# A decoder layer on one core: the block sums of the feed-forward weights are formed during attention and during the up product instead of during the input projection

## What is computed

```
z  = rmsnorm(x) @ w_in                      # 1024 x 3120
a  = GLA heads, sparse attention heads (three branches), mLSTM heads, from z
x  = x + concat(a) @ w_out                  # 1024 x 1024
x  = x + relu(rmsnorm(x) @ w_up)^2 @ w_down # 1024 x 4096, 4096 x 1024
```

## Time and profile before

| | us |
|---|---|
| Timed runs | 1925.2, 1925.57, 1929.59 (median 1925.57) |
| Profiled execution, its own time | 1918.35 |
| Its span, first to last instruction | 1916.6 |
| Projection | 0 to 517 |
| Attention | 517 to about 760 |
| Other mixers and the decoded samples | about 760 to 1110 |
| Output projection | about 1113 to 1228 |
| Up phase | about 1228 to 1573 |
| Down phase | about 1573 to the end |

### The profile page before, as it was taken

How to read it: one execution, slowest core, us unless ns; L and a number is a source line. 1 busy time by engine, 2 the same in 40 slices (tenths; PEclk the granted TensorE clock), 3 DMA queues, 4 the chain that set the end, 5 groups by cost and what they waited for, 6 DMA issues and landing times. The chain is left out here.

```text
span 1916.6 us, 34635 instructions
## 1 busy us (share of the span) xinstructions
PE 1694.0 (88%) x13909; PEld 1558.6 (81%) x13909; DVE 1091.9 (57%) x1814; ACT 736.7 (38%) x1379; POOL 261.9 (14%) x276
## 2 busy tenths in 40 slices
PE   7725998678799999799999779779999989999998
PEld 6625997678688888678876369779999989999998
DVE  6305326521278777556667775876666675545542
ACT  6311223110166555544445432343333343333331
POOL 1101000000122222332221132410000000000000
PEclk9866998798889999899999789989999999999999
DMA  7998889999941001357749756236556578665652
GB/s 171 151 300 202 154 165 283 283 225 204 226 100 24 2 2 44 117 202 244 235 148 271 167 171 196 75 117 218 175 186 189 182 247 285 184 200 185 196 174 62
DMA packets 339037, 333.61 MB, mean 174 GB/s; under 512 B 62190, under 2 KB 272710, under 8 KB 336254
## 3 DMA queue, kind: packets, MB, share of 16 engines
q1 hardware_dynamic: 309102, 226.20, 41.4%
q0 software_dynamic: 27392, 100.67, 20.0%
q10 hardware_dynamic: 2384, 4.53, 0.7%
HBM read 261.50 MB, written 141.15 MB: 210 GB/s over the span
## 5 line engine op out<-in xcount | busy, mean ns | idle before, releaser
L59 PE MATMUL pm<-ops,slots 128*128 128x258 f32 x1792 | 511.1, 285 | 26.6 <-DVE ops L3694 19.5
L60 PE MATMUL pm<-ops,slots 128*128 128x258 f32 x1792 | 509.4, 284 | 0.0
L61 PE MATMUL pm<-ops,slots 128*128 128x258 f32 x1792 | 508.3, 284 | 0.0
L59 PEld LDWEIGHTS pm<-ops,slots 128*128 128x128 f32 x1792 | 340.6, 190 | 27.6 <-DVE ops L3694 20.2
L61 PEld LDWEIGHTS pm<-ops,slots 128*128 128x128 f32 x1792 | 342.9, 191 | 0.0
L60 PEld LDWEIGHTS pm<-ops,slots 128*128 128x128 f32 x1792 | 342.8, 191 | 0.0
L59 PE MATMUL pz<-hH,winH 128*128 128x344 f32 x600 | 209.9, 350 | 60.7 <-DVE zb L910 59.0
L3521 ACT ACTIVATE slots<-uact 128x512 fp32r<-128x512 f32 x224 | 137.4, 626 | 172.7 <-DMA uact<-upS_scratch 48.0
L60 PE MATMUL pz<-hL,winH 128*128 128x344 f32 x600 | 201.8, 336 | 0.0
L61 PE MATMUL pz<-hH,winL 128*128 128x344 f32 x600 | 201.0, 335 | 0.0
L3700 DVE TENSOR_TENSOR slots<-uact,slots 128x512 fp32r<-128x512 f32 x224 | 156.5, 708 | 75.5 <-ACT slots L3521 75.4
(11 more groups left out here) (671 smaller groups left out, 3232.5 us busy)
## 6 DMA issues: line engine op xcount, KB each, us to landing
hidD_scratch<-onat SPq DMA_DIRECT2D x112, 258.0 KB, 3.8
upS_scratch<-in_w_up_dram POOLq DMA_DIRECT2D x12, 2048.0 KB, 21.5
downS_scratch<-in_w_down_dram POOLq DMA_DIRECT2D x12, 2048.0 KB, 17.1
hs<-hidD_scratch SPq DMA_DIRECT2D x38, 516.0 KB, 4.8
uact<-upS_scratch SPq DMA_DIRECT2D x64, 256.0 KB
uact<-downS_scratch SPq DMA_DIRECT2D x64, 256.0 KB
raw<-in_w_in_dram SPq DMA_DIRECT2D x24, 512.0 KB, 14.9
uact<-in_w_up_dram SPq DMA_DIRECT2D x48, 256.0 KB
```

The costliest lines, as they stand in the source:

```text
L59: nc.tensor.matmul(out, wH, mH, start=start and k == 0, stop=False)
L60: nc.tensor.matmul(out, wH, mL, start=False, stop=False)
L61: last = nc.tensor.matmul(out, wL, mH, start=False, stop=stop and k == n - 1)
```

## The change

All of the sums leave the projection. The sums of `w_up` are issued by POOL at the beginning of attention, behind the masks and before the first scaling step: four copies (eight DMAs) and the first adds of sums 0 and 1 there, the adds of sums 2 and 3 at the sliding steps one half and three quarters of the way through. The sums of `w_down` are issued by POOL in `mix_and_mixer` behind `x_fourth(1)`, when the second half's operands have been split; SP waits for each of them only where the down phase loads its first unit. The pacing by `raw_in` is gone. For `w_down` the rows are at most 512 bytes instead of 2048 (`max_dma_last_dim` counts bytes).

```diff
@@ project_and_prepare, gpsimd @@
-                for which in range(2):
-                    ...
-                    slot(1)
-                    begin(0, block_of(1, 0))
-                    slot(2)
-                    begin(1, block_of(0, 0))
-                    slot(3)
-                    begin(2, block_of(0, 0))
-                    slot(4)
-                    begin(3, block_of(0, 1))
-                    for n in range(2):
-                        slot(5 + n)
-                        add(0, n, block_of(1, 1))
-                    ...
@@ attend_prompt, gpsimd @@
+                def copy_sum(f, block):
+                    for n in range(2):
+                        rows = slice(n * 256, (n + 1) * 256)
+                        nc.gpsimd.dma_start(io["upS"][f, rows, :], block[rows, :], max_dma_last_dim=2048).then_inc(sums_done[f], 16)
+
+                def add_sum(f, block):
+                    pool.wait_ge(sums_done[f], 32)
+                    for n in range(2):
+                        rows = slice(n * 256, (n + 1) * 256)
+                        nc.gpsimd.dma_start(io["upS"][f, rows, :], block[rows, :], accum_op=ALU.add, max_dma_last_dim=2048).then_inc(sums_done[f], 16)
+                ...
+                copy_sum(0, up_quarter(1, 0))
+                copy_sum(2, up_quarter(0, 0))
+                copy_sum(1, up_quarter(0, 0))
+                copy_sum(3, up_quarter(0, 1))
+                add_sum(0, up_quarter(1, 1))
+                add_sum(1, up_quarter(1, 0))
+                sliding = [s for s in range(len(sched.steps)) if sched.steps[s][1] == WIN]
                 for s in range(len(sched.steps)):
+                    if s == sliding[len(sliding) // 2]:
+                        pool.wait_ge(sums_done[0], 64)
+                        add_sum(2, io["upS"][0])
+                    if s == sliding[3 * len(sliding) // 4]:
+                        pool.wait_ge(sums_done[2], 64)
+                        add_sum(3, io["upS"][2])
                     if s == ahead_at:
                         gather_ahead()
@@ mix_and_mixer, sync @@
                 def load_weights(n):
                     ...
+                    if n >= NUP and (n - NUP) % 16 == 0 and (n - NUP) // 16 in SUM_OF:
+                        sp.wait_ge(down_summed[SUM_OF[(n - NUP) // 16]], 64)
@@
                 for n in range(4):
-                    sp.wait_ge(late_sums[0][n], 64)
+                    sp.wait_ge(late_sums[n], 64)
@@
-                for n in range(4):
-                    sp.wait_ge(late_sums[1][n], 64)
@@ mix_and_mixer, gpsimd, behind x_fourth(1) @@
                 pool.wait_ge(xL_ready, 14)
+                ...
+                def copy_sum(f, block):
+                    for n in range(2):
+                        rows = slice(n * D, (n + 1) * D)
+                        nc.gpsimd.dma_start(io["downS"][f, rows, :], block[rows, :], max_dma_last_dim=512).then_inc(down_summed[f], 16)
+                (add_sum the same way, with accum_op=ALU.add and a wait for the sum's copy)
+
+                copy_sum(0, down_quarter(1, 0))
+                copy_sum(2, down_quarter(0, 0))
+                add_sum(0, down_quarter(1, 1))
+                copy_sum(1, down_quarter(0, 0))
+                pool.wait_ge(down_summed[0], 64)
+                add_sum(2, io["downS"][0])
+                copy_sum(3, down_quarter(0, 1))
+                add_sum(1, down_quarter(1, 0))
+                pool.wait_ge(down_summed[2], 64)
+                add_sum(3, io["downS"][2])
```

More of the change, by code:

```diff
@@ L77 @@
 QK_ROWS = (4, 5, 0, 1, 2, 3)
-SUM_ROW = 2048
 def project_and_prepare(nc, io, keep):
@@ L86, in project_and_prepare @@
     xTd = io["xT"].rearrange("(k p) t -> p k t", p=P)
-    w_up, w_down = io["w_up"].rearrange("l d n -> (l d) n"), io["w_down"].rearrange("l f n -> (l f) n")
     zT, zS = io["zT"], io["zS"]
@@ L1347, in _, with up_quarter @@
                 nc.gpsimd.memset(cmask[:, :, NB:P], -BIG).then_inc(masks, 1)
+                sums_done, w_up = keep["weight_sums"], io["w_up"].rearrange("l d n -> (l d) n")
+                def up_quarter(i, j):
+                    return w_up[j * 512:(j + 1) * 512, i * 2 * D:(i + 1) * 2 * D]
+                def copy_sum(f, block):
[7 more added lines that the diff above has]
+                        nc.gpsimd.dma_start(io["upS"][f, rows, :], block[rows, :], accum_op=ALU.add, max_dma_last_dim=2048).then_inc(sums_done[f], 16)
                 def scale_sliding(s):
@@ L3084, in mix_and_mixer @@
         acc_in = [sem(f"acc_in{m}") for m in range(NM)]
+        down_summed = [sem(f"down_summed{n}") for n in range(4)]
         smp_ready, out_t, out_a, ys_t, ys_a = (sem(n) for n in ("smp_ready", "out_t", "out_a", "ys_t", "ys_a"))
@@ L3335, in _, with down_quarter, add_sum @@
                 pool.wait_ge(xL_ready, 14)
+                w_rows = io["w_down"].rearrange("l f n -> (l f) n")
+                def down_quarter(i, j):
+                    return w_rows[j * 2 * D:(j + 1) * 2 * D, i * 512:(i + 1) * 512]
+                def copy_sum(f, block):
+                    for n in range(2):
+                        rows = slice(n * D, (n + 1) * D)
+                        nc.gpsimd.dma_start(io["downS"][f, rows, :], block[rows, :], max_dma_last_dim=512).then_inc(down_summed[f], 16)
+                def add_sum(f, block):
+                    pool.wait_ge(down_summed[f], 32)
+                    for n in range(2):
+                        rows = slice(n * D, (n + 1) * D)
+                        nc.gpsimd.dma_start(io["downS"][f, rows, :], block[rows, :], accum_op=ALU.add, max_dma_last_dim=512).then_inc(down_summed[f], 16)
+                copy_sum(0, down_quarter(1, 0))
[8 more added lines that the diff above has]
+                add_sum(3, io["downS"][2])
                 for j in FINAL:
@@ L3941, in program @@
             keep["late_z"] = nc.alloc_semaphore("late_z_stored")
-            keep["weight_sums"] = [[nc.alloc_semaphore(f"sums_{which}{n}") for n in range(4)] for which in ("up", "down")]
+            keep["weight_sums"] = [nc.alloc_semaphore(f"up_sums{n}") for n in range(4)]
             project_and_prepare(nc, io, keep)
```

## The result

The changed kernel took 1906.9 us in the median of five runs (1895.28 to 1916.99), the kernel before 1925.57 (1923.12 to 1930.35). The forecast of 1919 with 1870 to 1990 holds it, 12 us too high. The spans of the two profiled executions differ by 23.0 us, and all that follows takes that difference apart.

The account below looks back on a forecast made before the run. It took `raw` loads sharing DMA engines with the sums to bound the projection, PE attention and the up phase. -110 + 33 + 3 + 67 = -7 us gave 1911, or 1919 on the median's scale; range 1870 to 1990.

Parts of the forecast that it names:

- Step 1: Projection: without the sums its `raw` loads quicken and PE sets the pace, -110 us (bounds -130 to -75).
- The dear bound: Projection: the least gain, -75 us, if all 44 us of other waits stay and DVE adds 20.
- Step 2: Start of attention: POOL held until sum 1's copy lands, +33 us, and +3 for later adds.
- The hold: Start of attention: POOL's first scaling delayed by waiting for sum 1's copy, 32 us, taken as 33.
- the two later pairs: Attention: two later pairs of adds stop POOL 3.5 us each, mostly hidden, +3 us (0 to 7).
- Step 3: Up phase: packets of the `w_down` sums take turns with SP's weight loads, +67 us.
- loss less cover: Up phase, copies: loss of 37 us, less 11 us covered by units split ahead.
- loss less joins: Up phase, accumulates: loss of 49 us, less 8 for software-queue gaps at the joins of the chain.
- Accumulates of 2 KB: Rival, up phase: accumulates not made smaller or as dear as large ones, loss 97 to 134 us; chance 0.25.
- Copies that shrink: Rival, up phase: copy packets shrink too and cost nothing, loss about 20 to 38 us; chance 0.17.
- Another chain in the projection: Rival: `store_qk`, DVE's order or output stores keep slots near 14 us, return only 75, sum +28; chance 0.08.

Follow-up runs that it names:

- e5: Changed kernel with the first adds of `w_up` sums 0 and 1 moved to the 9th and 17th sliding step: 1858.21 us, ratio 0.9724 to the kernel before.
- e1: Changed kernel with all sums left out, plain quarters read instead (output not the layer's): 1790.1 us, ratio 0.9329 to the kernel before.
- e9: Changed kernel without `w_up` sums and with only the eight copies of the `w_down` sums, no adds: 1823.26 us, ratio 0.9511 to the kernel before.
- e4: Changed kernel with rows of 2048 instead of 512 bytes for the `w_down` sums: 1945.67 us, ratio 1.0129 to the kernel before.
- e3: Changed kernel with the `w_up` sums left out, plain quarters read instead: 1864.48 us, ratio 0.9724 to the kernel before.
- e6: Kernel before with 512-byte instead of 2048-byte rows in its accumulates, all sums still in the projection: 1954.22 us, ratio 1.0202.
- e7: Kernel before with `w_up` sums spread over projection slots (512-byte accumulate rows), `w_down` sums over attention's sliding steps, none in the up phase: 1798.54 us, ratio 0.9395.

## Why the prediction came out as it did

**What bounded the kernel** was read rightly: with the sums gone, `raw` lands in 3.6 us and PE is full.

**Step 1, -127.5 against -110.** The mechanism was right, the term mis-sized. The work of PE was put at 285 and measured at 288.45; the 25 us of waits that I kept on top of it are 3.5 us (292 - 288.45). Those waits in the profile before (9.1, 8.0, 7.5, 19.7) went with the sums, all but a few microseconds, although none of them was named for a DMA. The value lies inside the bounds of -130 to -75, near the end that I did not take. This term is more than the whole error of -16 in the span. (The dear bound has a slip: 285 + 44 + 20 against 420 is -71, not -75.)

**Step 2, +37.6 against +36.** Right in its cause: the adds behind the wait for sum 1's copy were issued at 446.2, 56.7 behind the masks, and PE waited 40.0 us for it; e5 takes the wait away and gets all of it back. That the size is right too is partly luck, since two misses cancel. The hold was put too low: the first scaling came 39 us later than before (58.7 behind the masks, not 19.5), where 32 stood. A pair took 10 x 16 / 606 = 0.264 us in 415:425, not 0.204, and 6 x 32 of them make 51 us; sum 1's copy landed 52.7 us after POOL began (393.2 to 445.9), where 44 stood. SP's packets there were of 1.13 MB / 605 = 1.9 KB: the query and key loads have rows of 4 KB and 2 KB (8 and 4 times 128 elements, line 3910 of the kernel before), not of 512 bytes as the section on attention says. And the 3 us for the two later pairs are not seen: e5 has them too and its stretch is e1's.

**Step 3, +65.3 against +67.** Right in its mechanism and, partly by luck, in the sum; the 65.3 are also those of the fastest run. The pair of an accumulate was put at 0.093 and measured at 0.0937. The parts were off against each other: the copies cost 35 to 37 us by e9 where loss less cover made 26, the accumulates 34 to 41 where loss less joins made 41. The copies' transfers took longer than 55 us, from 1134 to 1202 in e9, at 0.240 a packet in place of 0.215, though SP passed 1.6 packets for each, not one. All transfers took 309 us and not the forecast 245: POOL issued the second of a pair only when the first had landed, so there was a gap of the software queue at each of them. SP never waited for `down_summed` at a price: the last accumulate landed at 1482.4, the first down load was issued at 1529.3, and the down phase has 364.3 us against 362.7.

**The rivals.** Accumulates of 2 KB: refuted by the packets (512 bytes), and e4, which has such packets, shows that its price was right (114 us where 97 to 134 stood). Copies that shrink: refuted by the 4 KB packets of 512-byte rows. The Trainium skill (DMA: Bandwidth & Descriptors, SWDGE vs HWDGE vs iDMA) says that a software packet is preferably of at most 4096 bytes. The packets of the sums agree with that here; the copies' reach it (2.58 MB / 646), the accumulates' stop at their row (2.09 MB / 4100). Another chain in the projection: refuted by PE's 288.45 of 292 us.

**The chances.** They leaned to slower (0.47 against 0.41), though the sum was on the faster side, because a quarter was given to packets of 2 KB for accumulates. The trace before had shown no accumulate packet above its row, with room for two; that was the better evidence, and 0.25 was too much for the rival.

**What stays open.** The kernel after has wider runs (21.7 us, 1.1%) than the kernel before beside it (7.2 us; up to 13.7 in the later batches). Variants with down sums in the up phase spread by 8.2 to 16.4 us (e3, e4, e5, e9), the others by 2.1 to 4.5; what does it was not tried. Neither was why a 512-byte accumulate is held on POOL until the one before has landed; the profile has only "issue" there. With rows of 2048 (e4) POOL issues two 0.8 us apart.

## What to carry to other kernels

Background transfers belong where the foreground's loads are shorter than its compute by more than they add, one 2 MB half per slot here: spread over projection and attention the same sums cost 10 to 13 us where they cost 130 in the projection alone. When a transfer must share the engines, ask for the size of its packet before its bytes: here the up phase lost 114 us with rows of 2048 bytes and 65 with rows of 512, for the same bytes. An issue with a wait in the program of an engine that feeds the bound is worth as much as the wait, and it is moved by a few lines; and when a wait for one resource is removed, the smaller waits near it can go too, as 44 us of them became 3.5 here.

## What the runs showed of the hardware

- An accumulating DMA keeps its row as its packet: 512-byte rows gave 512-byte packets (0.0937 us for a pair with SP's packet), 2048-byte rows 2 KB ones (0.208, e4). A copy fills 4 KB from rows of either size.
- Small rows relieve the other queue and burden the issuer: an accumulate of 2 MB to `downS` in 512-byte rows holds POOL 2.9 to 4.9 us, against 1.27 in the kernel before with 2048, and the next such accumulate was issued only 0.3 to 0.4 us behind its landing, 17 to 34 us later (kernel after and e6).
- The turns are one to one in stretches (606 to 605 packets in the kernel after, 846 to 848 in e4), but over e9's copies of 512-byte rows SP had 1.6 packets to one, from 385 to 380 in one piece to 652 to 1332 in another. Whether the software queue was short of packets there, no run shows.
- In 400:440 PE had 8.26 us of work and a granted clock of 0.50 (the 1.2 GHz level), in e7 34.21 us of work and 0.87, a mean over both levels.
